# Sums of squares by head in the first block: two products in rounded fp32 in place of one full fp32 product

## The chip, the cores and the metric

The kernel runs on one core of a Trainium2 chip. The metric is the time on the device of one launch, in microseconds (us). An engine of the core is written as the profile writes it: PE is the matrix engine TensorE (PEld its weight loads), DVE is VectorE, ACT is ScalarE, POOL is GpSimd, SP issues the transfers of weights.

## The reference

512 tokens of width 1024 go through two blocks. The change touches the first one, whose queries and keys are normalized head by head before the attention:

```python
proj = rmsnorm(x, ln1_g) @ w_in
qa, ka, va, qb, kb, vb, ga, gb = split(proj)
qa = rope(rmsnorm_by_head(qa, q_norm_a))      # 12 heads of 64, as ka
qb = rope(rmsnorm_by_head(qb, q_norm_b))      # 8 heads of 64; kb has 2
oa = dilated_attention(qa, ka, va)
ob = banded_attention(qb, kb, vb, 127, sinks)
mix = sigmoid(ga) * (oa @ w_branch_a) + sigmoid(gb) * (ob @ w_branch_b)
x = x + mix @ w_out
# then x + relu(rmsnorm(x) @ w_up)**2 @ w_down, and a second block of another kind
```

`rmsnorm_by_head` divides each head's 64 values by the root of their mean square, in fp32.

## The kernel before

Activations lie transposed: a tile has 128 features on the partitions and 512 tokens beside each other. A "head" of the program (`head_chain`) is one such tile with two heads of 64 in it. There are 17 in the first block: one for kb, four for qb, six each for qa and ka.

**The dense work** is done with numbers split in two: weights and activations are each rounded to a high part (type fp32r) and the rest is kept as a low part, and a block of 128x128 weights costs three products of 128x512 (high by high, high by low, low by high). A group, 8 blocks and 24 products, makes one tile of a projection. Weights come by transfer in units of 8 blocks; ACT rounds the unit (`half_weights`, L1679), POOL subtracts in four quarters (L1992), and PE waits for each quarter. Group by group the result is taken from the bank by DVE (`proj`, L1197).

**A head** goes through these steps. `head_in`: DVE multiplies by gain and cosine (L1203) and shuffles a copy (L1204), while ACT squares the tile (L1749). `head_sum`: PE multiplies the squares by `bones`, a 128x128 matrix of ones in two blocks of 64, which puts each head's sum on all of its rows; it is one product in full fp32. `head_rope`: DVE, L1211 and L1213. `head_rs`: ACT takes logarithm, exponential and square (L1710, L1712, L1715). `head_newton`: DVE, L1219 and L1222. `head_out`: POOL multiplies (L2000). The chain has three tiles and two banks for itself, a **slot**, and there are three slots.

**Attention** works in the same three slots. 16 items of banded attention (`swa_item`, four query tiles by four blocks of rows) each take scores, softmax (DVE L1282, L1285 and three tiny steps from L1288, then L1298, L1301 and L1305 twice), a transposition (L875), values and a copy (L1310). 8 dilated items (`dil_item`) are some three times as large (L1246, L1252, L1262, L1270 on DVE, L841 on PE), and the first four need all of six heads, the last four all of six others.

**The order of the work** is made when the program is built. `Schedule` keeps a clock for each engine by costs of its own, puts a slot's next step into the program as soon as its inputs would be there, and puts dense groups between. A free slot takes the next head if one waits, and only otherwise an attention item:

```python
def fill(self):
    for i, g in enumerate(self.slots):
        queue = self.side if i == len(self.slots) - 1 else self.heads or self.waiting
```

The dense groups of this stage are the 17 tiles of the heads and 16 gates. The gates are kept back where their tiles lie on memory that attention still uses:

```python
for k in range(2):
    gate1(k)
sch.until(*[(n, t_) for n in ("qa", "ka") for t_ in (1, 3, 5)])
heads_done = tuple(slot_head.values())
for k in range(2, 11):
    gate1(k, heads_done)
```

In the same way the gates 11 to 13 wait in the order for `until("oa0")`, the first four dilated items, gate 14 for `until("oa")`, all eight, and gate 15 for the last attention item. On the chip each engine goes through its instructions in the order that was planned, whatever the real times are.

## Time and profile before

| | us |
|---|---|
| median of 3 runs (lowest, highest) | 2407.05 (2406.53, 2407.55) |
| profiled execution, span | 2406.4 |
| PE busy | 2379.8 (99%) |
| PEld busy | 1924.6 (80%) |
| DVE busy | 1209.2 (50%) |
| ACT busy | 965.8 (40%) |
| POOL busy | 1316.2 (55%) |

The span of the profiled execution is its time from first to last instruction, 0.7 us under the median. The page cuts it into 40 slices of 60 us. PE is busy in nine tenths of each slice but the first; the granted clock is full in all of them (mean 0.998). DVE has 5 in the first slice, then 9 and 9, then 7, and between 2 and 7 afterwards. The first block's attention runs from 58 to 330 us. The chain of work that ended last is 91% PE, 6% DVE.

### The profile page before, as it was taken

Reading aid. Unit: us, or ns where it says so; the run is one execution under the profiler, and the core shown is the slowest. Engines: PE = TensorE matmul, PEld = TensorE weight load, DVE = VectorE, ACT = ScalarE, POOL = GpSimd, SP = SyncE. Lnnn points to the kernel's source line nnn. Section 1 sums busy time; section 2 is a strip of 40 time slices with the busy share of each in tenths; the row PEclk is TensorE's granted clock in tenths of the full one; section 3 lists DMA queues with packets and bytes.
Section 4 is the critical chain, followed back from the end, with each engine's and each line's share of the span. In section 5 each row is a group of like instructions: output and inputs, shape, how many; then the busy total and the mean of one; then the engine's idle time right before and its main releaser. Section 6 shows DMA issues by size and latency. Waiting matters only on the chain.

```text
span 2406.4 us, 29717 instructions
## 1 busy us (share of the span) xinstructions
PE 2379.8 (99%) x11108; PEld 1924.6 (80%) x11108; DVE 1209.2 (50%) x1961; ACT 965.8 (40%) x1513; POOL 1316.2 (55%) x1589
## 2 busy tenths in 40 slices
PE   8999999999999999999999999999999999999999
PEld 8777778888888888777787888888887777788887
DVE  5997765423224432379625743333325785266331
ACT  4554444322223223566524432332336764344321
POOL 5763246656556655366244765555554562466554
PEclk9999999999999999999999999999999999999999
DMA  5321123333333333222122333333332221223333
GB/s 166 109 71 53 47 77 97 96 97 97 97 97 110 97 97 103 71 72 69 54 87 79 97 97 97 96 97 97 97 98 67 72 78 53 88 87 98 96 97 96
DMA packets 59758, 213.40 MB, mean 89 GB/s; under 512 B 6624, under 2 KB 6752, under 8 KB 59488
## 3 DMA queue, kind: packets, MB, share of 16 engines
q1 hardware_dynamic: 59472, 211.38, 29.2%
q8 instruction: 88, 1.44, 0.2%
q14 instruction: 54, 0.44, 0.1%
q10 hardware_dynamic: 144, 0.14, 0.0%
HBM read 209.39 MB, written 2.10 MB: 88 GB/s over the span
## 4 chain that ended last, share of the span: by engine, by line
PE 91%; DVE 6%; issue 1%; ACT 1%; DMA 0%; POOL 0%; SPq 0%; DVEq 0%; ACTq 0%
PE banks L721 89%; DVE t L1203 1%; DVE t L1211 1%; DVE t L1213 1%; DVE t L1488 1%; DVE t L1204 1%; DVE t L1197 1%; DVE t L1219 0%; PE banks L841 0%; PE banks L995 0%; DVE t L1222 0%; ACT t L1679 0%; DMA t<-in_w 0%; PE banks L875 0%; POOL t L1992 0%
## 5 line engine op out<-in xcount | busy, mean ns | idle before, releaser
L721 PE MATMUL banks<-t,t 128*128 128x512 f32 (+4 forms) x10788 | 2351.7, 387 | 17.2 <-ACT t L1699 5.9
L721 PEld LDWEIGHTS banks<-t,t 128*128 128x128 f32 (+2 forms) x10788 | 1889.5, 188 | 452.2 <-issue 64.3
L1992 POOL TENSOR_TENSOR t<-t,t 128x256 fp32r<-128x256 f32 x1544 | 1258.9, 846 | 1049.9 <-ACT t L1679 1041.5
L1679 ACT ACTIVATE t<-t 128x1024 fp32r<-128x1024 f32 x385 | 408.2, 1060 | 1078.8 <-issue 605.5
L1197 DVE TENSOR_TENSOR t<-banks,t 128x512 f32<-128x512 f32 x121 | 83.1, 687 | 169.8 <-PE banks L721 169.2
L1378 DVE TENSOR_TENSOR t<-banks,t 128x512 f32<-128x512 f32 x44 | 30.4, 690 | 184.5 <-PE banks L721 184.3
L1346 DVE SCALAR_TENSOR_TENSOR t<-banks,t 128x512 f32<-128x512 f32 x32 | 22.1, 691 | 155.4 <-PE banks L721 155.4
L1080 DVE SCALAR_TENSOR_TENSOR t<-t,t,t 128x512 fp32r<-128x512 f32 x64 | 52.0, 817 | 58.1 <-ACT t L1699 58.1
L1323 DVE TENSOR_TENSOR t<-t,t 128x512 fp32r<-128x512 f32 x68 | 70.5, 1036 | 2.3
L1352 DVE TENSOR_TENSOR t<-banks,t 128x512 f32<-128x512 f32 x24 | 16.6, 691 | 106.0 <-PE banks L721 106.0
L1699 ACT ACTIVATE t<-t,t 128x512 fp32r<-128x512 f32 x64 | 45.6, 715 | 55.7 <-DVE t L1346 49.1
L2000 POOL TENSOR_TENSOR t<-t,t 128x512 f32<-128x512 f32 x33 | 49.6, 1506 | 29.7 <-DVE t L1222 29.7
L1373 DVE TENSOR_TENSOR t<-banks,t 128x512 f32<-128x512 f32 x44 | 30.4, 691 | 70.3 <-PE banks L721 69.9
L1093 DVE TENSOR_TENSOR t<-t,t 128x512 f32<-128x512 f32 x56 | 59.4, 1061 | 3.1 <-ACT t L1705 3.1
L1321 DVE CAST t<-t 128x512 fp32r<-128x512 f32 x68 | 55.3, 813 | 2.5
L1358 DVE SCALAR_TENSOR_TENSOR t<-banks,t 128x512 f32<-128x512 f32 x32 | 22.1, 691 | 65.2 <-PE banks L721 65.1
L1344 DVE TENSOR_TENSOR t<-banks,t 128x512 f32<-128x512 f32 x32 | 22.1, 690 | 56.6 <-PE banks L721 56.6
L1488 DVE SCALAR_TENSOR_TENSOR t<-t,t,t 128x511 f32<-128x511 f32 (+2 forms) x48 | 46.7, 972 | 7.1 <-ACT t L1887 6.3
L1715 ACT ACTIVATE t<-t 128x512 f32<-128x512 f32 x45 | 28.5, 633 | 33.4 <-DVE t L1213 32.5
L1710 ACT ACTIVATE t<-banks,t 128x512 f32<-128x512 f32 x45 | 30.6, 681 | 22.5 <-PE banks L721 22.4
L1098 DVE SCALAR_TENSOR_TENSOR t<-banks,t 128x512 f32<-128x512 f32 x12 | 8.3, 692 | 57.8 <-ACT t L1715 57.7
L1705 ACT ACTIVATE t<-t 128x512 f32<-128x512 f32 x56 | 34.6, 617 | 4.8 <-DVE t L1093 4.8
(182 smaller groups left out, 1304.7 us busy)
## 6 DMA issues: line engine op xcount, KB each, us to landing
t<-in_w SPq DMA_DIRECT2D x386, 512.0 KB, 3.5
t<-in_xT SPq DMA_DIRECT2D x8, 256.0 KB, 5.7
out<-t SPq DMA_DIRECT2D x8, 256.0 KB, 4.5
t<-in_dmask SPq DMA_DIRECT2D x1, 1536.0 KB, 7.7
t<-in_vbias SPq DMA_DIRECT2D x2, 384.0 KB, 4.1
t<-in_c SPq DMA_DIRECT2D x1, 576.0 KB, 8.6
t<-in_w SPq DMA_DIRECT2D x2, 256.0 KB, 3.9
t<-in_pos SPq DMA_DIRECT2D x2, 256.0 KB, 4.1
```

Source lines behind the costliest of these rows:

```text
L721: return pe.matmul(o, l, r, start=start, stop=stop, skip_group_check=True)
L1080: v.scalar_tensor_tensor(out=XL[m], in0=X[m], scalar=g, in1=as_f32(XH[m]), op0=M_, op1=S_).then_inc(*v_norm.next(("xl", s, m)))
L1093: v.tensor_tensor(acc, acc, sqt, A_).then_inc(*v_norm.next(("acc", s, m)))
L1197: v.tensor_tensor(G.dst, B[G.bank], rstdB, M_).then_inc(*v_evac.next(("proj", g)))
L1321: v.tensor_copy(hi, src).then_inc(*v_evac.next())
L1323: v.tensor_tensor(lo, src, as_f32(hi), S_).then_inc(*v_evac.next(name))
L1488: v.scalar_tensor_tensor(out=dst[:, tap:S], in0=T[k][:, 0:S - tap], scalar=cols_t[:, cw + 3 - tap:cw + 4 - tap], in1=dst[:, tap:S], op0=M_ ...
L1679: a.activation(whl[u % 2][:, 0:1024], wraw[u % 3][:, :], ACT.Copy).then_inc(*w_high.next(u))
L1699: a.activation(XH[m], X[m], ACT.Copy, scale=col(STAGE[s], m)).then_inc(*a_norm.next(("high", s, m)))
L1705: a.activation(sqt, X[m], ACT.Square).then_inc(*a_norm.next(("square", s, m)))
L1992: p.tensor_tensor(hl[:, 1024:2048][:, c], wraw[u % 3][:, c], as_f32(hl[:, c]), ALU.subtract).then_inc(*w_low.next((u, q)))
L2000: p.tensor_tensor(H["R"], b_, a, ALU.mult).then_inc(*p_attn.next(("head", hid)))
```

## The change

For the 17 heads of the first block ACT squares the tile twice: once to fp32, as before, and once rounded to fp32r (`SQH`). DVE subtracts the two and writes the rest as fp32r (`SQL`), a new step `head_split`. PE then makes two products with a rounded copy of `bones`, one for each part, into the same bank. The copy of `bones` is made once on DVE in `turns1`, in memory that the second block's `consts` fills later; `consts` waits for the 17 sums. `SQH` and `SQL` lie in the slot's attention tiles. The second block's heads (gains of table 2) stay as they were.

```diff
+        SQH = [reg(88 + 6 * s, S, F32R)[:, :] for s in range(3)]
+        SQL = [reg(91 + 6 * s, S, F32R)[:, :] for s in range(3)]
+        bones_r = mask_r[:, 0:128]
...
             def head_sum(hid):
                 H = heads[hid]
                 ba = pair(H["slot"])[0]
+                if H.get("table") == 1:
+                    need.wait_ge(*v_norm.at(("bones",)))
+                    need.wait_ge(*a_attn.at(("square_high", hid)))
+                    need.wait_ge(*v_attn.at(("square_low", hid)))
+                    free(ba)
+                    mm(B[ba], bones_r, SQH[H["slot"]], True, False)
+                    mm(B[ba], bones_r, SQL[H["slot"]], False, True).then_inc(*t_attn.next(("sum", hid)))
+                    bank[ba] = [(v_attn, ("summed", hid))]
+                    return
...
+                v.tensor_copy(bones_r, C["bones"]).then_inc(*v_norm.next(("bones",)))
...
+            def head_split(hid):
+                H = heads[hid]
+                a = H["tiles"][H["slot"]][0]
+                need.wait_ge(*a_attn.at(("square_high", hid)))
+                reach(need, *H["tile_free"])
+                v.tensor_tensor(SQL[H["slot"]], a, as_f32(SQH[H["slot"]]), S_).then_inc(*v_attn.next(("square_low", hid)))
...
                 a.activation(a_, H["R"], ACT.Square).then_inc(*a_attn.next(("square", hid)))
+                if H["table"] == 1:
+                    reach(need, *H["tile_free"])
+                    a.activation(SQH[H["slot"]], H["R"], ACT.Square).then_inc(*a_attn.next(("square_high", hid)))
...
-                put("head_in", hid)
-                yield "t", (a_attn, ("square", hid))
+                if k["table"] == 1:
+                    k["tile_free"] = list(slot_busy[slot])
+                    put("head_in", hid)
+                    yield "v", (a_attn, ("square_high", hid))
+                    put("head_split", hid)
+                    yield "t", (v_attn, ("square_low", hid))
+                else:
+                    put("head_in", hid)
+                    yield "t", (a_attn, ("square", hid))
                 put("head_sum", hid)
```

The planned order moves with it. The first place is DVE, between the evictions of two neighbouring groups (L1197, in the change L1212) in the middle of the heads. Before (the next eviction follows):

```order
L1197 TENSOR_TENSOR t_101<-banks,t_57 128x512
L1298 TENSOR_TENSOR t_67<-t_67 128x2
L1301 RECIPROCAL t_67<-t_67 128x2
L1305 TENSOR_SCALAR t_124<-t_124,t_67 128x256 x2
L1203 SCALAR_TENSOR_TENSOR t_167<-t_104,t_66,t_56 128x512
L1204 STREAM_SHUFFLE t_168<-t_104 128x512
L1310 COPY t_123<-banks 128x128
L1211 SCALAR_TENSOR_TENSOR t_168<-t_168,t_62,t_56 128x512
L1213 TENSOR_TENSOR t_167<-t_167,t_168 128x512
L1310 COPY t_64<-banks 128x128
L1203 SCALAR_TENSOR_TENSOR t_164<-t_110,t_66,t_56 128x512
L1204 STREAM_SHUFFLE t_165<-t_110 128x512
```

With the change (L1218 and L1219 are `head_in`, L1226 the subtraction, L1233 and L1235 `head_rope`, L1241 and L1244 `head_newton`):

```order
L1212 TENSOR_TENSOR t_101<-banks,t_57 128x512
L1233 SCALAR_TENSOR_TENSOR t_171<-t_171,t_62,t_56 128x512
L1235 TENSOR_TENSOR t_170<-t_170,t_171 128x512
L1226 TENSOR_TENSOR t_135<-t_172,t_132 128x512
L1212 TENSOR_TENSOR t_107<-banks,t_57 128x512
L1241 SCALAR_TENSOR_TENSOR t_171<-banks,t_171 128x512
L1244 SCALAR_TENSOR_TENSOR t_169<-t_171,t_169 128x512
L1233 SCALAR_TENSOR_TENSOR t_174<-t_174,t_62,t_56 128x512
L1235 TENSOR_TENSOR t_173<-t_173,t_174 128x512
L1218 SCALAR_TENSOR_TENSOR t_167<-t_110,t_66,t_56 128x512
L1219 STREAM_SHUFFLE t_168<-t_110 128x512
L1212 TENSOR_TENSOR t_103<-banks,t_57 128x512
```

The attention steps between them (L1298 to L1310) have moved to behind the heads; from the first eviction to the last `head_newton` five banded items have passed their copy L1310 before, and one with the change.

The second place is PE, around the last head's sum, just ahead of gate 2. Dense products are `t_50` with `t_54` or `t_55`. Before, a head's sum is `t_160`, `t_163` or `t_166` with `t_58`, the scores of banded items are `t_117` with another, those of dilated ones `t_106`, and L875 is a transposition:

```order
L721 MATMUL banks<-t_166,t_58 128x512
L721 MATMUL banks<-t_50,t_55 128x512 x18
L721 MATMUL banks<-t_50,t_54 128x512 x3
L721 MATMUL banks<-t_163,t_58 128x512
L721 MATMUL banks<-t_50,t_54 128x512 x3
L721 MATMUL banks<-t_117,t_114 128x256 x2
L721 MATMUL banks<-t_50,t_54 128x512 x18
L721 MATMUL banks<-t_106,t_100 128x512 x2
L721 MATMUL banks<-t_160,t_58 128x512
L875 MATMUL banks<-t_58,t_128 128x128 x4
L721 MATMUL banks<-t_50,t_55 128x512 x15
L721 MATMUL banks<-t_129,t_118 64x128 x4
```

With the change a sum is a pair, `t_130` to `t_132` and then `t_133` to `t_135`, each with `t_63`; the last row is gate 2:

```order
L724 MATMUL banks<-t_131,t_63 128x512
L724 MATMUL banks<-t_134,t_63 128x512
L724 MATMUL banks<-t_132,t_63 128x512
L724 MATMUL banks<-t_135,t_63 128x512
L724 MATMUL banks<-t_117,t_114 128x256 x2
L724 MATMUL banks<-t_117,t_115 128x256 x2
L724 MATMUL banks<-t_130,t_63 128x512
L724 MATMUL banks<-t_133,t_63 128x512
L724 MATMUL banks<-t_50,t_55 128x512 x24
```

The sums of the last three heads now stand in a row, with no dense product between them. Ahead of the last sum there stood six scores, five transpositions and five values of banded items and one pair of a dilated item's scores; now it is three, one, one and none.

The third place is PE between gates 13 and 15. Before, from late in gate 13 on, the steps of the last banded items stand singly between dense rows, up to the first product of the branch outputs:

```order
L721 MATMUL banks<-t_50,t_54 128x512 x12
L875 MATMUL banks<-t_58,t_124 128x128 x4
L721 MATMUL banks<-t_50,t_55 128x512 x6
L875 MATMUL banks<-t_58,t_128 128x128 x4
L721 MATMUL banks<-t_117,t_116 128x256 x2
L721 MATMUL banks<-t_125,t_118 64x128 x4
L721 MATMUL banks<-t_129,t_118 64x128 x4
L721 MATMUL banks<-t_50,t_55 128x512 x18
L875 MATMUL banks<-t_58,t_126 128x128 x4
L721 MATMUL banks<-t_127,t_118 64x128 x4
L721 MATMUL banks<-t_50,t_54 128x512 x24
```

With the change, 134 products of attention stand in a row between gates 13 and 14, of which this is the beginning (`t_107` to `t_111` are scores of dilated items, L853 their transpositions, 64x128 their values). They hold the transpositions and values of four dilated items, all of the scores of one of these, and four scores, three transpositions and two values of banded items:

```order
L724 MATMUL banks<-t_50,t_54 128x512 x15
L853 MATMUL banks<-t_58,t_124 128x128 x4
L853 MATMUL banks<-t_58,t_125 128x128 x4
L853 MATMUL banks<-t_58,t_128 128x128 x4
L853 MATMUL banks<-t_58,t_129 128x128 x4
L853 MATMUL banks<-t_58,t_124 128x128 x2
L853 MATMUL banks<-t_58,t_125 128x128 x2
L724 MATMUL banks<-t_109,t_103 128x128 x2
L724 MATMUL banks<-t_111,t_105 128x128 x2
L853 MATMUL banks<-t_58,t_128 128x128 x2
L853 MATMUL banks<-t_58,t_129 128x128 x2
L724 MATMUL banks<-t_124,t_112 64x128
```

The longest row without a dense product had 48 before, between groups of gates. From the branch outputs on, the order is the same.

## Rows read from the trace of the kernel before

**Rows 1.** The page: busy time of the engines over the whole span.
```profile
PE 2379.8 (99%) x11108; PEld 1924.6 (80%) x11108; DVE 1209.2 (50%) x1961; ACT 965.8 (40%) x1513; POOL 1316.2 (55%) x1589
...
DVE  5997765423224432379625743333325785266331
```

**Rows 2.** Windows: heads, rest of attention, dense products; busy us by engine.
```profile
58.50:189.00 130.50, 126.20 (x554) 92.24 (x553) 121.76 (x195) 69.87 (x120) 89.30 (x88) 1.00 0.29 91
189.00:330.00 141.00, 138.47 (x890) 106.82 (x891) 100.22 (x235) 62.60 (x139) 43.71 (x58) 1.00 0.18 53
330.00:400.00 70.00, 70.00 (x310) 58.01 (x309) 45.97 (x59) 29.80 (x41) 45.36 (x52) 1.00 0.31 91
```

**Rows 3.** Order of time, PEld: weight loads around the first head's sum (start, us).
```profile
60.29 0.35 PEld L721 LDWEIGHTS banks<-t,t 128*128 128x128 f32 x2
60.88 0.19 PEld L721 LDWEIGHTS banks<-t,t 128*128 128x128 f32 x1 [0.24 <-issue]
61.31 0.42 PEld L721 LDWEIGHTS banks<-t,t 128*128 128x128 f32 x2 [0.24 <-issue]
```

**Rows 4.** Groups of instructions on DVE, 58.5 to 196.5 us (busy us, mean ns).
```profile
L1305 DVE TENSOR_SCALAR t<-t,t 128x256 f32<-128x256 f32 x12 | 8.0, 703 | 0.2
L1282 DVE SCALAR_TENSOR_TENSOR t<-banks,t 128x256 f32<-128x256 f32 x12 | 4.5, 411 | 0.0
L1285 DVE TENSOR_REDUCE t<-t 128x2 f32<-128x512 f32 x6 | 4.1, 686 | 0.2
L1298 DVE TENSOR_TENSOR t<-t 128x2 f32<-128x2 f32 x6 | 2.9, 480 | 0.0
L1288 DVE TENSOR_TENSOR t<-t,t 128x2 f32<-128x2 f32 x6 | 2.1, 358 | 0.2
L1310 DVE COPY t<-banks 128x128 f32<-128x128 f32 x6 | 1.6, 279 | 0.3 <-PE banks L721 0.3
```

**Rows 5.** Groups of instructions on ACT, 58.5 to 189 us: the squares.
```profile
L1749 ACT ACTIVATE t<-t 128x512 f32<-128x512 f32 x17 | 10.5, 617 | 0.7 <-POOL t L2000 0.5
```

**Rows 6.** One line, L1213, 60 to 330 us: duration in ns, min/median/max.
```profile
L1213 DVE TENSOR_TENSOR t<-t,t x17: 691/1110/1664, 61.9 to 192.2; 128x512 f32<-128x512 f32 x17
```

**Rows 7.** Order of time around the last head's sum, PEld.
```profile
188.84 0.30 PEld L721 LDWEIGHTS banks<-t,t 128*128 128x128 f32 x2 [0.66 <-ACT t L1749]
...
191.10 0.42 PEld L875 LDWEIGHTS banks<-t,t 128*128 128x128 f32 x4 [1.97 <-DVE t L1305]
...
191.49 2.15 PEld L721 LDWEIGHTS banks<-t,t 128*128 128x128 f32 x10
```

**Rows 8.** Order of time, PEld: a banded item's scores, then another's values.
```profile
91.55 0.30 PEld L721 LDWEIGHTS banks<-t,t 64*128 64x128 f32 x4 [0.35 <-issue]
92.18 0.30 PEld L721 LDWEIGHTS banks<-t,t 128*128 128x128 f32 x2 [0.33 <-issue]
...
137.84 0.42 PEld L721 LDWEIGHTS banks<-t,t 128*64 128x64 f32 x8 [0.17 <-issue]
138.43 1.00 PEld L721 LDWEIGHTS banks<-t,t 128*128 128x128 f32 x5 [0.17 <-issue]
```

**Rows 9.** Waits, 58.5 to 330 us (us in total, times, longest us).
```profile
POOL t L1992 <- ACT t L1679: 122.9, 27, 12.8
...
PEld banks L721 <- POOL t L1992: 0.7, 3, 0.2
```

**Rows 10.** Order of time: first and last step of the last dilated item.
```profile
290.80 1.29 DVE L1246 SCALAR_TENSOR_TENSOR t<-banks,t 128x512 f32<-128x512 f32 x2 [2.34 <-PE banks L721]
...
314.79 0.38 ACT L1791 ACTIVATE t<-banks 128x128 f32<-128x128 f32 x1
```

**Rows 11.** Groups of instructions on DVE, 189 to 330.2 us: dilated items.
```profile
L1252 DVE TENSOR_REDUCE t<-t 128x1 f32<-128x768 f32 x16 | 14.5, 947 | 0.3
L1262 DVE TENSOR_SCALAR t<-t,t 128x768 f32<-128x768 f32 x16 | 10.8, 672 | 0.6
L1246 DVE SCALAR_TENSOR_TENSOR t<-banks,t 128x512 f32<-128x512 f32 x16 | 10.2, 681 | 3.6 <-PE banks L721 3.6
```

More of the change, by code:

```diff
@@ L677, in build_program @@
         groups, stage_end, wide_of = [], {}, {}
-        heads = {}
+        heads, heads_first = {}, []
         dil_at, swa_at, gates1, merge1 = {}, {}, {}, {}
@@ L1114, in consts @@
                 need.wait_ge(*in_cols.at("cols"))
+                for hid in heads_first:
+                    need.wait_ge(*t_attn.at(("sum", hid)))
                 v.tensor_copy(mask_r[:, 0:128], C["ident"]).then_inc(*v_norm.next())
@@ L1644, in vector_program @@
                     "rope_angles": rope_angles, "values1": values1, "proj": proj, "head_in": head_in, "key_rope": key_rope,
-                    "head_rope": head_rope, "head_newton": head_newton, "dil_soft": dil_soft, "dil_norm": dil_norm,
+                    "head_split": head_split, "head_rope": head_rope, "head_newton": head_newton, "dil_soft": dil_soft, "dil_norm": dil_norm,
                     "dil_pt": dil_pt, "swa_soft": swa_soft, "swa_norm": swa_norm, "swa_out": swa_out,
@@ L2239, in head1 @@
             src = proj(n, 0, R, rope1)
+            heads_first.append((n, t_))
             sch.heads.append(head_chain((n, t_), R=R, g=col(n), table=1, turned=TURNED[n], ones=C["bones"], n=64,
```

## The prediction

> **What bounds the kernel now.** The page first: PE is busy in 99% of the span and DVE in 50%, but DVE's digits have two slices with a 9, from 60 to 180 us, which is where the heads are [rows 1]. So an average says little here, and the windows are read next. With the heads (58.5 to 189 us) PE is busy for 126.2 of 130.5 us and DVE for 121.8; in the rest of the attention (to 330 us) PE for 138.5 of 141.0, DVE for 100.2; behind that PE alone counts [rows 2]. The first stage thus has two engines that are both nearly full, and the change takes work from one and gives it to the other.
>
> **What PE gains.** The loads around the first head's sum show a full fp32 product as two loads: the first begins 0.19 us before the end of its row, at 60.45, the second at 60.88, and the next dense product's at 61.31, so it takes 0.86 us [rows 3]. A dense product, of the same type and size as each of the two new ones, takes 70.0 / 310 = 0.226 us [rows 2]. Per head 0.86 - 0.45 = 0.41 us, for 17 heads 6.9 us less on PE. That would be the whole story if PE alone counted.
>
> **What ACT and POOL get.** ACT gets 17 squares of 0.62 us [rows 5], 10.5 us, beside 69.9 us of work in 130.5 [rows 2]. It has room, and the square stands early in a chain that is over 10 us long; three slots need to give a head only every 7.7 us (130.5 / 17). I cost it at nothing. If that cover goes, weights are rounded later, since they stand behind it on ACT. POOL gets nothing, but waits 122.9 us for ACT's rounding between 58.5 and 330 us, and PE waited for POOL for only 0.7 us [rows 9], so a late square of 0.6 us is taken up there.
>
> **What DVE gets in the stage of the heads.** 17 subtractions of two tiles of 128x512 that both lie in SBUF. The nearest row is L1213, same size and kind: 0.69 at least, 1.11 median, 1.66 at most [rows 6]. I take the median: 18.9 us. The cast of `bones` and one shuffle that now comes before the last sum are together about 1 us. But the order also takes work out of this stage. Five softmax fronts go behind the heads (L1282 twice, L1285 and three tiny steps, no longer than L1288: 0.82 + 0.69 + 1.07 = 2.58 us each), four backs (L1298 and L1305 twice: 1.89 us) and four copies (0.28 us) [rows 4]: 12.9 + 7.5 + 1.1 = 21.5 us. Net, DVE has 18.9 + 1.0 - 21.5 = -1.6 us up to the last head's sum. Its stage took 130.5 us for 121.8 us of work [rows 2], so by the same ratio the last sum, at 188.84 us before [rows 7], comes about **2 us earlier**. With the subtraction at 0.69 us it would be 9 us earlier, with 1.66 us 8 us later; these are the bounds.
>
> So nothing of the 6.9 us is seen here. PE has 126.2 - 6.9 us less what was moved behind (next part), about 110 us of work, in a stage that DVE makes 128 us long: some 18 us of waiting, most of it where three sums stand in a row ahead of gate 2, with all dense products that may stand there used up.
>
> **What PE gets behind the heads.** The steps that were moved are three scores, four transpositions, four values of banded items and a pair of dilated scores. With the idle time ahead, scores take 0.35 + 0.63 us and values 0.17 + 0.59 us [rows 8]; a transposition takes 0.39 us [rows 7]; the dilated pair has no row and is taken as the scores. Together 2.9 + 1.6 + 3.0 + 1.0 = 8.5, so **+9 us** (6 us without the idle times, 11 us if each step costs 0.2 us more). In this stage PE was busy for 138.5 of 141.0 us [rows 2], so all of it shows.
>
> **The row of 134 products between gates 13 and 14.** Here PE has no dense product to fill with, and DVE sets the pace. DVE's work in it: of dilated items 8 times L1262, 4 times L1252 and 4 wide L1246 [rows 11] are 5.4 + 3.8 + 2.7 us; 4 narrower L1246 and 8 copies from the banks, taken as L1282 [rows 4], 4.9 us; four whole softmaxes and three copies of banded items, at most 4 x 4.47 + 0.8 = 18.7 us. In all at most 35.5 us; the banded part is priced by the crowded stage, so I take 33. The end of it runs beside gate 14 (24 x 0.226 = 5.4 us), which leaves 27 us to PE. PE's own work in it, by the durations above, is 19 us (60 transpositions at 0.39 per four, 56 values at 0.59 per four, 4 scores at 0.63 and 2 us for the dilated scores). So **+8 us** of waiting. Least is 0, as before nothing of this size shows there. Most is the chain: the fourth dilated item starts when the first has given its values, and the last one took 24.4 us from its scores' arrival to its end (290.80 to 315.17) [rows 10], with 7 us ahead of it 31 us, so +12.
>
> **Sum.** -2 + 9 + 8 = +15 us on the profiled execution's 2406.4, which lies 0.7 us under the median of 2407.05: **2422 us**, 0.6% slower. Everything behind 330 us stands in the same order and is taken as unchanged; `consts` waits for sums that are long past.
>
> **A rule against my price.** The rows show L1213 at 0.69 or at 1.11 us and more, with nothing in between explained by its size [rows 6]. The Trainium skill, page "SBUF — State Buffer", section "SBUF: two separate sides", says that VectorE and GpSimd share a pair of ports that is locked for a whole instruction when VectorE has two inputs in SBUF, and that the loser waits. That fits a subtraction that often waits for one of POOL's quarters. By the rule the added subtraction makes POOL wait as well, and its price is 0.69 us plus luck; this gives the second rival below.
>
> **Rivals.**
> *Faster: only PE counts.* -6.9 us, 2400 us. It decides if DVE's queue up to the last sum is done within PE's own 110 us, and the row between gates 13 and 14 within PE's 19. For it: PE is the bound of the page. Against: DVE's 121.8 us of work less 1.6 us [rows 2], which would have to shrink by 10 us. Chance 0.05.
> *Cheap subtraction.* At 0.69 us each the last sum comes 9 us earlier: -9 + 9 + 8 = +8, 2415 us. For it: the least duration of the row, and that the order leaves fewer instructions to collide with. Chance 0.17.
> *The moved work fits.* Cheap subtraction, and DVE keeps up in the row of 134 products: -9 + 6 + 0 = -3 to +3, about 2407 us. For it: DVE has 40 us free behind the heads [rows 2]. Against: they are not in that row. Chance 0.09.
> *Collisions.* The subtraction at its dearest, POOL's quarters and so the weights late, the chain at its longest: +8 + 9 + 12 = +29, 2436 us. For it: three waits in a row on an engine that is full. Against: POOL waits for ACT so much [rows 9]. Chance 0.13.
> *The change isn't what it says*, one of the two products takes as long as a full one: 17 x 0.4 us more on PE, in a stage where PE waits anyway. It moves the time by less than the bounds do, and every dense product [rows 2] speaks against it.
>
> **How the numbers follow.** The forecast has 0.56. A measurement can tell about 0.2%, 4.8 us, from no change. Faster by more than that is only the first rival: 0.05. Within it is most of the case in which the moved work fits: 0.08. The rest, 0.87, is slower. The range takes in the cheap subtraction and nearly all of the collisions: 2409 to 2435 us.
>
> **What would show it.** Right: the last pair of products for a head at about 187 us; PE busy for some 110 of 130 us in the stage of the heads, its waits ended by DVE's subtraction; the new DVE line with 17 instructions of 1.0 to 1.1 us; gate 13 evicted near 305 us and gate 14 some 33 us later; PE's waits there ended by DVE; the first product of the branch outputs at about 345 us in place of 330; the same 2076 us behind it. Wrong: if PE doesn't wait in the heads, the step on DVE's queue fails; if the row of 134 products runs in 20 us, the third term fails; if the time behind the branch outputs moves, something isn't here at all.

## The result and the profile after

| | before | after |
|---|---|---|
| median (lowest, highest) of 4 runs each, us | 2406.79 (2405.76, 2407.55) | 2427.26 (2426.25, 2428.98) |
| profiled execution, span, us | 2406.4 | 2424.6 |

The change makes the kernel slower: 1.0081 times the time before, with an interval from 1.0069 to 1.0093; the medians lie 20.5 us apart. The forecast was 2422, with 2409 to 2435 as its range. All medians here and below are of fast runs, so one run of 9181 us (of e11) and one of 3937 us (of e12) are left out of them.

The page of the kernel after, busy time over the whole span and DVE's digits. Against [rows 1] PE is busy as long as before, which is one per cent less of the span; PE's line in the costliest groups now shows 31.2 us of idle time where it showed 17.2.

```profile
PE 2380.2 (98%) x11108; PEld 1928.3 (80%) x11108; DVE 1218.8 (50%) x1979; ACT 975.3 (40%) x1530; POOL 1324.6 (55%) x1589
...
DVE  5996766423224432378634843333325785266330
...
L724 PE MATMUL banks<-t,t 128*128 128x512 f32 (+5 forms) x10788 | 2349.5, 386 | 31.2 <-ACT t L1771 6.1
```

The windows of [rows 2], for the kernel after (the columns are window, its length, busy time and instructions of PE, PEld, DVE, ACT and POOL, granted clock, DMA share, GB/s):

```profile
58.50:189.00 130.50, 115.88 (x492) 89.52 (x491) 123.03 (x169) 71.22 (x110) 99.40 (x92) 0.95 0.30 94
189.00:330.00 141.00, 130.85 (x838) 99.00 (x836) 101.23 (x252) 62.52 (x150) 37.34 (x49) 0.98 0.15 46
330.00:400.00 70.00, 68.48 (x334) 56.02 (x335) 46.24 (x75) 30.05 (x49) 33.70 (x40) 0.98 0.23 69
```

With the heads PE is busy for 10 us less than before and DVE for 1 us more. Behind them PE has waits where it had nearly none.

Four moments of DVE's queue say where the time went: the first head's eviction, the last step of the last head (`head_newton`), and the evictions of gates 13, 14 and 15. In order of time, before:

```profile
58.61 0.69 DVE L1197 TENSOR_TENSOR t<-banks,t 128x512 f32<-128x512 f32 x1 [2.72 <-PE banks L721]
...
195.71 0.69 DVE L1222 SCALAR_TENSOR_TENSOR t<-t,t 128x512 f32<-128x512 f32 x1
...
313.58 0.69 DVE L1197 TENSOR_TENSOR t<-banks,t 128x512 f32<-128x512 f32 x1
...
322.18 0.69 DVE L1197 TENSOR_TENSOR t<-banks,t 128x512 f32<-128x512 f32 x1 [0.99 <-PE banks L721]
...
330.21 0.69 DVE L1197 TENSOR_TENSOR t<-banks,t 128x512 f32<-128x512 f32 x1 [0.49 <-PE banks L721]
```

and after:

```profile
58.21 0.69 DVE L1212 TENSOR_TENSOR t<-banks,t 128x512 f32<-128x512 f32 x1 [2.72 <-PE banks L724]
...
193.52 0.69 DVE L1244 SCALAR_TENSOR_TENSOR t<-t,t 128x512 f32<-128x512 f32 x1
...
301.09 0.69 DVE L1212 TENSOR_TENSOR t<-banks,t 128x512 f32<-128x512 f32 x1 [0.33 <-PE banks L724]
...
342.04 0.69 DVE L1212 TENSOR_TENSOR t<-banks,t 128x512 f32<-128x512 f32 x1 [2.12 <-PE banks L724]
...
350.05 0.69 DVE L1212 TENSOR_TENSOR t<-banks,t 128x512 f32<-128x512 f32 x1 [0.47 <-PE banks L724]
```

Two stretches are read from them for every run below. **Heads** is first eviction to last newton: 137.1 us before, 135.3 after, so -1.8. **Behind** is last newton to gate 15: 134.5 before, 156.5 after, so +22.0. Inside it the way to gate 13 is 10.3 us shorter and the stretch from gate 13 to 14 grows from 8.6 to 41.0 us. What follows gate 15 takes 2076.2 and 2074.6 us.

The waits of the kernel after in the heads' stage (us in total, times, longest):

```profile
PEld banks L724 <- ACT t L1771: 7.2, 3, 5.5
PE banks L724 <- ACT t L1771: 6.1, 2, 5.1
...
PE banks L724 <- DVE t L1226: 5.7, 6, 1.8
```

The first two rows name ACT's plain square (L1771), which no sum of the change waits for: a sum waits for the rounded square (L1774) and the subtraction (L1226) of its own head. The longest of these waits, in order of time, shows what it was:

```profile
174.44 0.62 ACT L1774 ACTIVATE t<-t 128x512 fp32r<-128x512 f32 x1
...
178.93 1.20 DVE L1226 TENSOR_TENSOR t<-t,t 128x512 fp32r<-128x512 f32 x1
...
179.64 0.61 ACT L1771 ACTIVATE t<-t 128x512 f32<-128x512 f32 x1
...
180.16 0.61 ACT L1774 ACTIVATE t<-t 128x512 fp32r<-128x512 f32 x1
180.25 0.50 PEld L724 LDWEIGHTS banks<-t,t 128*128 128x128 f32 x2 [5.47 <-ACT t L1771]
```

The head's rounded square was there at 175.06. The squares at 179.64 and 180.16 are the next head's; the second of them ended at 180.77, when PE was already at work. What this sum waited for is its subtraction, which ended at 180.13, as in the other wait put down to L1771 (the subtraction ended at 165.76, the load began at 165.88). So 5.7 + 6.1 = 11.8 us of PE's waits with the heads are ended by the subtraction.

The chain of work that ended last, in the row without dense products, shows how that row runs (start us, us, what):

```profile
301.89 0.62 DVE t L1284
...
308.89 1.81 DVE t L1274 x2
310.70 0.67 DVE t L1292 x2
311.42 2.71 PE banks L724 x28
314.13 1.02 PE banks L853 x8
...
319.26 1.81 DVE t L1274 x2
...
321.38 0.63 DVE t L1327 x2
```

It passes from DVE to PE and back, since an item's transposition, softmax and values each wait for the step before. Nothing stands between for PE to do meanwhile.

### The profile page after: what moved, and what is told of

It reads as the page before. It is cut to its first block, busy times and chain, and to the rows that moved or that the text cites. A ratio compares the mean times of both kernels' runs of the same rounds, so it can differ in the third digit from the quotient of the medians.

```text
span 2424.6 us, 29769 instructions
## 1 busy us (share of the span) xinstructions
PE 2380.2 (98%) x11108; PEld 1928.3 (80%) x11108; DVE 1218.8 (50%) x1979; ACT 975.3 (40%) x1530; POOL 1324.6 (55%) x1589
## 4 chain that ended last, share of the span: by engine, by line
PE 88%; DVE 3%; issue 1%; ACT 1%; POOL 1%; DVEq 0%; ACTq 0%
PE banks L724 86%; PE banks L853 0%; PE banks L1007 0%; POOL t L2017 0%; PE banks L887 0%; DVE t L1218 0%; ACT t L1701 0%; DVE t L1510 0%; POOL t L2025 0%; DVE t L1244 0%; DVE t L1233 0%; DVE t L1212 0%; DVE t L1219 0%; DVE t L1235 0%; PE banks L1063 0%
## 5 line engine op out<-in xcount | busy, mean ns | idle before, releaser
L724 PE MATMUL banks<-t,t 128*128 128x512 f32 (+5 forms) x10788 | 2349.5, 386 | 31.2 <-ACT t L1771 6.1
L1212 DVE TENSOR_TENSOR t<-banks,t 128x512 f32<-128x512 f32 x121 | 83.0, 686 | 165.8 <-PE banks L724 163.8
```

The source lines that it names most:

```text
L724: return pe.matmul(o, l, r, start=start, stop=stop, skip_group_check=True)
L1212: v.tensor_tensor(G.dst, B[G.bank], rstdB, M_).then_inc(*v_evac.next(("proj", g)))
```

## The experiments

Two theories stood at first. **D**: VectorE's time paces the heads' stage, as predicted. **O**: what counts is the order, in two ways, TensorE standing in order at a head's sum, and attention steps driven behind the heads. A third, **P**, is that each microsecond of TensorE's work counts. Here are all 12 kernels, each with its ratio to the kernel before in runs on the same chip (its median there was 2408.19 us beside e1 to e4, 2406.72 beside e5 to e8, 2407.71 beside e9 to e12) and the two stretches read as above, in us:

| run | us, median | ratio (interval) | heads | behind |
|---|---|---|---|---|
| before | 2406.79 | | 137.1 | 134.5 |
| the change | 2427.26 | 1.0081 (1.0069 to 1.0093) | 135.3 | 156.5 |
| e1_old_order | 2441.19 | 1.0138 (1.0125 to 1.0152) | 165.9 | 137.2 |
| e2_full_product | 2431.87 | 1.0101 (1.0086 to 1.0117) | 136.3 | 158.1 |
| e3_high_part_only | 2415.30 | 1.0026 (1.0016 to 1.0037) | 129.4 | 148.4 |
| e4_pool_subtracts | 2453.69 | 1.0189 (1.0175 to 1.0203) | 150.5 | 167.4 |
| e5_work_not_awaited | 2417.34 | 1.0050 (1.0036 to 1.0064) | 146.5 | 136.3 |
| e6_longer_chain | 2413.72 | 1.0028 (1.0017 to 1.0039) | 141.7 | 135.5 |
| e7_filled_waits | 2428.66 | 1.0089 (1.0075 to 1.0102) | 135.5 | 155.3 |
| e8_subtract_at_once | 2426.87 | 1.0080 (1.0067 to 1.0093) | 133.4 | 157.0 |
| e9_new_order_alone | 2423.53 | 1.0067 (1.0054 to 1.0079) | 131.5 | 157.0 |
| e10_relieved_before | 2403.85 | 0.9986 (0.9977 to 0.9995) | 133.5 | 135.4 |
| e11_relieved_old_order | 2437.55 | 1.0125 (1.0110 to 1.0141) | 164.2 | 138.9 |
| e12_high_part_old_order | 2411.65 | 1.0014 (1.0005 to 1.0023) | 137.6 | 138.0 |

### Old order, full product, high part alone, GpSimd

**e1_old_order**: the planner doesn't see the new steps, so they stand in the order of the kernel before.

```diff
                if k["table"] == 1:
                     k["tile_free"] = list(slot_busy[slot])
                     put("head_in", hid)
-                    yield "v", (a_attn, ("square_high", hid))
                     put("head_split", hid)
-                    yield "t", (v_attn, ("square_low", hid))
+                    yield "t", (a_attn, ("square", hid))
```

> All instructions of the change, but in the order of before: the planner is given no time for the second square and the subtraction and the old time for the sum, so each engine's instructions stand as before, with the new ones put in. Theory D (DVE's queue paces the heads): DVE has the 17 subtractions, 18 us, in the stage of the heads and nothing is moved out of it, so the last head's sum comes some 13 us later than before (about 202 us); behind it PE has the same work as before and no bare row, so the whole is +13 us, about 2420 us, some 7 us under the change. Rival O (the moved order alone costs): with the old order the time is that of before or up to 7 us under it, 2400 to 2407 us.

Measured: 33 us over the kernel before, 28.8 of them in the heads' stage. Both theories missed it: D had +13 us, O at most none. VectorE's work alone doesn't explain it. In the waits, from 58.5 to 227 us:

```profile
PE banks L724 <- DVE t L1238: 24.4, 13, 3.0
DVE t L1221 <- PE banks L724: 21.0, 13, 2.8
```

PE stands at 13 sums for the subtraction (L1238), up to 3.0 us each; then DVE stands for the evictions of products (L1221) that PE made late because of it. Two queues in order lose the same time in turn.

**e2_full_product**: the change and its order, with one full fp32 product in place of the two (the planner still reckons with the two).

```diff
-                    mm(B[ba], bones_r, SQH[H["slot"]], True, False)
-                    mm(B[ba], bones_r, SQL[H["slot"]], False, True).then_inc(...)
+                    mm(B[ba], H["ones"], H["tiles"][H["slot"]][0]).then_inc(...)
```

> The change with its squares, subtractions and order, but PE makes the old full fp32 product of the fp32 squares at the place of the two products; the rounded parts are made and waited for, not used. So PE gets its 17 x 0.4 = 6.9 us back. Theory D: PE waits for more than that in the stage of the heads, so 0 to +3 us against the change, about 2429 us. Rival P (each us of PE counts): +7 us, 2434 us.

Measured: 4.6 us over the change by the medians, 3.2 if each is taken against the kernel before in its own series. In the profiled executions 1.0 us lies in the heads' stage and 1.6 behind; the rest is in the start of the first head, which differs between 58 and 61 us from kernel to kernel, and in the tail. So of TensorE's 6.9 us some 2.5 are seen in the two stretches. The medians alone don't part D's bound of 3 from P's 7, since the two intervals overlap; the stretches speak for D.

**e3_high_part_only**: one product of the rounded square, no subtraction. It leaves out the low part of the squares.

```diff
-                    need.wait_ge(*v_attn.at(("square_low", hid)))
                     free(ba)
-                    mm(B[ba], bones_r, SQH[H["slot"]], True, False)
-                    mm(B[ba], bones_r, SQL[H["slot"]], False, True).then_inc(...)
+                    mm(B[ba], bones_r, SQH[H["slot"]]).then_inc(...)
```

> Leaves out the low part: ACT makes the rounded square alone, no subtraction, one product per head, so the sums are those of rounded squares. PE has 17 x 0.63 = 10.7 us less than before, DVE and ACT have the same as before. Theory D: DVE's queue still paces the heads, so of the 10.7 us only 0 to 4 are seen; about 2404 us. Rival P: -10.7 us, 2396 us.

Measured: 7 us slower than before, against both expectations, though TensorE has 10.7 us less to do and VectorE only the cast of `bones` more. The heads' stage is 7.7 us shorter, the stretch behind it 13.9 longer: the planner, told of cheaper sums, wrote another order again. This run turned the study to the order.

**e4_pool_subtracts**: the subtraction on GpSimd.

```diff
-                v.tensor_tensor(SQL[H["slot"]], a, as_f32(SQH[H["slot"]]), S_).then_inc(*v_attn...)
+                p.tensor_tensor(SQL[H["slot"]], a, as_f32(SQH[H["slot"]]), ALU.subtract).then_inc(*p_attn...)
```

> The change, but POOL makes the subtraction (some 1.5 us each, 25 us beside 89 us of its work in the stage of the heads). DVE is relieved of 18 us, but the planner moves all banded items behind the heads and leaves the same row of 134 products without a dense one. Theory D with its second part (moved work and the bare row cost by themselves): the last sum comes 5 us or more earlier than with the change (under 182 us), the rest of the attention costs as much or 2 us more, so 2420 to 2427 us. Rival: if DVE's added 18 us are all there is, 2405 to 2410 us.

Measured: 26 us over the change, outside both expectations, with VectorE free for a third of the stage. VectorE's busy time doesn't set this stage: PE stands for 21.2 us at three sums for GpSimd's subtraction, which waits behind GpSimd's quarters of the weights. From the start of `head_in` on VectorE to the end of `head_out` on GpSimd a head takes 24.2 us, the mean of 17 (17.1 in the change, 11.8 before). That a long chain costs by itself isn't shown: in e8 the mean is 14.7 us at the change's time, and in e9 it is 17.0 us with a shorter heads' stage than before.

### The work, the chain, the clock, the place in the queue

**e5_work_not_awaited**: order and products of the kernel before; rounded square, difference and cast are done, but no sum waits for them.

```diff
                 if H.get("table") == 1:
-                    need.wait_ge(*a_attn.at(("square_high", hid)))
-                    need.wait_ge(*v_attn.at(("square_low", hid)))
+                    need.wait_ge(*a_attn.at(("square", hid)))
...
-                v.tensor_tensor(SQL[H["slot"]], a, as_f32(SQH[H["slot"]]), S_)
+                v.tensor_tensor(SQL[H["slot"]], as_f32(SQH[H["slot"]]), as_f32(SQH[H["slot"]]), S_)
```

> The kernel before and its order, with all the work that the change adds put in where it would stand in that order (the rounded square on ScalarE, a difference of two 128x512 tiles on VectorE behind each of the 17 heads' first two VectorE instructions, the cast of bones), but nobody waits for any of it: the heads' sums stay full fp32 products of the plain square, behind the plain square alone. It tells what the work costs by itself. Theory D (VectorE's time paces the heads' stage): 17 x 1.11 = 19 us of VectorE work are added to 122 of 130 us and nothing is moved out, so some +13 us on the kernel before. Theory O (the run with the old order lost its 33 us to TensorE standing in order at each sum for the subtraction, and the change loses its 20 us to the new order): 0 to +5 us.

Measured: +10.6 us, +9.4 in the heads' stage. The group of the difference, 58.5 to 210 us:

```profile
L1230 DVE TENSOR_TENSOR t<-t 128x512 fp32r<-128x512 f32 x17 | 11.9, 701 | 0.8 <-ACT t L1780 0.8
```

It was cheaper than the 1.11 us of D's sum. If all of the 9.4 us come from it, four fifths of its 11.9 us show, and VectorE's queue paces that stage in the old order; ScalarE's 17 added squares are in the same run and were not parted from it. Of e1's 33 us some 10.6 are the work, and some 22 come only when the sum waits for it.

**e6_longer_chain**: the kernel before with two more squares on ScalarE ahead of the awaited one.

```diff
+                if H["table"] == 1 and not isinstance(a, Planned):
+                    a.activation(SQH[H["slot"]], H["R"], ACT.Square)
+                    a.activation(SQL[H["slot"]], H["R"], ACT.Square)
                 a.activation(a_, H["R"], ACT.Square).then_inc(*a_attn.next(("square", hid)))
```

> The kernel before and its order, with two more squares on ScalarE ahead of the one that a head's sum waits for: each head's chain is longer by 2 x 0.62 = 1.2 us on ScalarE, which has 60 us free in this stage; no work is added to VectorE, TensorE or GpSimd, and the order is as it was. It leaves out nothing. If the length of a head's chain alone decided in a given order (theory O, TensorE stands in order at each sum): at most 17 x 1.2 = +20 us, less where a sum was not late. If VectorE's time decides (D): within 2 us of the kernel before, since the sum stands far enough behind the square.

Measured: +7 us, +4.6 in the heads' stage, for 1.2 us more in each of 17 chains on an engine that has room. D alone would have given nothing. So work on ScalarE ahead of a head's awaited square isn't free. (In the change the added square stands behind the plain one.)

**e7_filled_waits**: the change with dummy dense products in PE's waits.

```diff
+            def filler(n, bk):
+                free(bk)
+                for i in range(n):
+                    mm(B[bk], XH[0][:, 0:128], XH[0])
...
+                    filler(FILL_SUM.get(fill["sums"], 0), ba)
                     need.wait_ge(*a_attn.at(("square_high", hid)))
```

> The change, with dummy products of the dense kind (0.226 us each) put where TensorE waited in the change's profile: 37 ahead of the last four heads' sums (2.1, 5.5, 2.8 and 0.8 us of waiting there) and 48 in the row without dense products between gates 13 and 14; they write banks that are free and are overwritten, nothing else reads them. They measure what the lowered granted clock behind the waits costs (0.50 at 180 to 190 us and 0.83 at 320 to 340 us in the change's profile). If the waits are all that is lost and the clock matters little: the change's time within 2 us, or up to 4 us longer where a filler is still running when its wait would have ended. If the lowered clock stretched the work behind the waits: the granted clock stays near 1 in those windows and the time falls by some 3 to 6 us, to 2421 to 2424.

Two windows, 170 to 180 us and from gate 13 to 14, of PE alone (window, length, busy time, granted clock, DMA share, GB/s), first of the change:

```profile
170.00:180.00 10.00, 3.46 (x15) 0.82 0.23 71
301.00:342.00 41.00, 30.94 (x243) 0.92 0.05 14
```

then of e7:

```profile
170.00:180.00 10.00, 10.00 (x45) 1.00 0.33 105
301.00:342.00 41.00, 40.36 (x295) 1.00 0.05 14
```

PE is now busy without a break and at full clock there, and the time is the change's (+1.4 us, inside both intervals). PE's waits are what the row's length leaves over, and neither they nor the lowered clock made it: those 41 us belong to the chains over DVE and ACT. The first expectation holds. In the heads' stage the dummy products took half of the waits (PE idle for 7.1 us in place of 14.6) and the stage was as long (135.5 against 135.3). From 180 to 190 us PE was busy for only 6.84 us and the clock fell to 0.74, so there a cost of the clock stays untested.

**e8_subtract_at_once**: the subtraction right behind the head's first two instructions on VectorE.

```diff
                     put("head_in", hid)
-                    yield "v", (a_attn, ("square_high", hid))
                     put("head_split", hid)
```

> The change, but the subtraction is put into VectorE's queue right behind the head's first two instructions and not as a step of its own: a head's chain has one turn in VectorE's queue less, VectorE may instead stand and wait for ScalarE's rounded square. The same operations, the planner sees them. If the length of the chains (three slots held longer) is what drives steps behind the heads and so the time: chains shorter than the change's 17.1 us, more banded steps ahead of the last sum, and 3 to 10 us faster than the change. If VectorE's time is what counts: the same or 0 to 5 us slower, since VectorE now also waits.

Measured: the change's time (-0.4 us); 1.9 us gained with the heads, 0.5 lost behind, the rest at the start. A head's chain is 14.7 us in place of 17.1. Neither the turn in VectorE's queue nor the length of the chain is what costs here.

### The order alone, and relief

**e9_new_order_alone**: the order is planned for the change, the operations issued are those of the kernel before.

```diff
-                if H.get("table") == 1:
+                if H.get("table") == 1 and PLANNING[0]:
                     need.wait_ge(*v_norm.at(("bones",)))
...
             def head_split(hid):
+                if not PLANNING[0]:
+                    return
...
-                if H["table"] == 1:
+                if H["table"] == 1 and PLANNING[0]:
                     reach(need, *H["tile_free"])
                     a.activation(SQH[H["slot"]], H["R"], ACT.Square).then_inc(...)
```

> The change's order of steps on every engine, with the operations of the kernel before in it: each head has its one plain square and its full fp32 product, there is no rounded square, no subtraction and no cast of bones. It leaves out nothing. It tells what the new order costs by itself. From the run with the high part alone (new order of its own, no VectorE work, 8.6 us over the kernel before), and since the heads' stage loses 19 us of VectorE work: last head's sum 6 to 9 us earlier than in the kernel before, the stretch behind it some 18 us longer; +8 to +12 us in all, and so the work and its waits in that order are the other 8 to 12 of the change's 20. If the order is harmless and the work alone counts: -8 to 0.

Measured: +15.8 us, more than the 8 to 12 expected, so 15.8 of the change's 20.5 us come with the order alone. (The two intervals overlap a little; the stretches below place the rest.) Behind the heads it is the change again (157.0 against 156.5). In order of time, gates 13 and 14:

```profile
297.87 0.69 DVE L1224 TENSOR_TENSOR t<-banks,t 128x512 f32<-128x512 f32 x1 [0.33 <-PE banks L735]
...
338.77 0.69 DVE L1224 TENSOR_TENSOR t<-banks,t 128x512 f32<-128x512 f32 x1 [2.12 <-PE banks L735]
```

40.9 us, as in the change. The heads' stage is 5.6 us shorter than before, though VectorE is busy in it for 13 us less (115.2 against 128.3), and the chain of work from 58.5 to 189 us says why: in the kernel before

```profile
by line: PE banks L721 28.7%; DVE t L1203 9.2%; DVE t L1211 9.1%; DVE t L1213 7.5%; DVE t L1219 6.3%; DVE t L1204 6.2%; issue 6.0%; DVE t L1222 4.8%; DVE t L1197 4.8%; POOL t L1992 3.1%; ACT t L1715 2.0%; DVE t L1305 2.0%; DVE t L1282 1.6%;
```

and in e9

```profile
by line: PE banks L735 86.2%; issue 3.3%; POOL t L2031 2.5%; DVE t L1230 2.1%; DVE t L1247 1.4%; POOL t L2039 1.3%; DVE t L1231 1.1%; ACT t L1715 0.8%; DVE t L1249 0.6%; DVE t L1255 0.5%; PE banks L898 0.3%; DVEq L214 0.0%
```

With the moved steps gone from VectorE, TensorE becomes the bound for most of the stage (busy for 124.0 of 131.5 us), so only 5.6 us are gained. The change then puts 17.2 us of subtractions on VectorE and takes 6.9 from TensorE: 3.8 us back, which is the rest of its loss but for a microsecond.

**e10_relieved_before**: VectorE's product by the sine table over 64 of 512 columns, in the kernel before. It leaves out that part of the rotation, and so does the next.

```diff
-                v.scalar_tensor_tensor(out=c, in0=c, scalar=H["turned"], in1=SIN, op0=M_, op1=M_)...
+                n_ = 64 if H["table"] == 1 and not isinstance(v, Planned) else 512
+                v.scalar_tensor_tensor(out=c[:, 0:n_], in0=c[:, 0:n_], scalar=H["turned"], in1=SIN[:, 0:n_], op0=M_, op1=M_)...
```

> The kernel before and its order, but VectorE's product of the turned head by the sine table (1.17 us on 128x512) runs over 64 of the 512 columns: VectorE has 17 x 1.0 = 17 us less to do in the heads' stage. It leaves out that part of the rotation. It is the base for the run with the same relief and the change's operations. If VectorE's time paces the stage (D): 5 to 10 us faster, then TensorE (126 of 130 us) is the bound. If the chains' turns in a fixed order decide (O): 0 to 3 us faster.

Measured: -3.9 us. The groups of that line, 58.5 to 196 us, of the kernel before and of e10:

```profile
L1211 DVE SCALAR_TENSOR_TENSOR t<-t,t,t 128x512 f32<-128x512 f32 x17 | 19.9, 1170 | 0.4
```

```profile
L1212 DVE SCALAR_TENSOR_TENSOR t<-t,t,t 128x64 f32<-128x64 f32 x17 | 12.3, 721 | 0.4
```

An eighth of the columns took six tenths of the time, so the relief was 7.6 us and not 17. It shortened the heads' stage by 3.6 us, half of what was taken away, and the run by 3.9, between the 0 to 3 of O and the 5 to 10 that D expected for 17 us.

**e11_relieved_old_order**: the same relief in e1 (same edit as e10).

> The run e1_old_order (all operations of the change, in the order of the kernel before, +33 us) with the relief of e10_relieved_before: VectorE's product by the sine table over 64 of 512 columns, so that VectorE has as much work as in the kernel before. It leaves out that part of the rotation. D (the 33 us come from VectorE's queue being late at each sum): within 5 us of the kernel before, 8 to 12 us over e10. O (TensorE stands at each sum for one more turn of a chain, however full VectorE is): 20 us and more over e10, 2418 or more.

Measured: +29.8 us over before, 33.7 over e10; the relief took 1.6 us from e1's heads' stage. With the relief smaller than meant D's test is weaker, but its 8 to 12 us over e10 is far off: TensorE's standing in order at the sums is what e1 pays for, as O says.

**e12_high_part_old_order**: the order of the kernel before, one rounded square, one one-pass product. It leaves out the low part of the squares.

```diff
-                mm(B[ba], H["ones"], H["tiles"][H["slot"]][0]).then_inc(...)
+                mm(B[ba], *((bones_r, SQH[H["slot"]]) if H.get("table") == 1 and not PLANNING[0] else (H["ones"], ...))).then_inc(...)
...
+                if H["table"] == 1 and not PLANNING[0]:
+                    reach(need, *H["tile_free"])
+                    a.activation(SQH[H["slot"]], H["R"], ACT.Square).then_inc(*a_attn.next(("square", hid)))
```

> The order of the kernel before on every engine; for the 17 heads one rounded square in place of the plain one and one one-pass product in place of the full fp32 product, and nothing on VectorE but the cast of bones. It leaves out the low part of the squares, which the sum of squares then lacks. TensorE has 17 x (0.86 - 0.23) = 10.7 us less to do and no chain is longer. It tells what TensorE's gain is worth where nothing is given for it. If VectorE paces the stage (D, the prediction's step): 0 to -3 us on the kernel before. If TensorE does: -8 to -11 us.

Measured: +3.9 us (1.0014, interval 1.0005 to 1.0023), so no gain and a small loss, outside both expectations. TensorE's 10.7 us buy nothing, and the heads' stage stays at 137.6 us, as D's step has it; PE only stands longer in it (13.4 us idle in place of 5.4). The loss shows behind the heads, 138.0 against 134.5. PE alone in that stretch, before and in e12:

```profile
195.71:330.21 134.50, 133.11 (x864) 1.00 0.18 52
197.63:335.61 137.98, 136.59 (x881) 1.00 0.17 51
```

It has 17 products more to do there at full clock, at 0.226 us each 3.8 us: products that PE had done before the last newton in the kernel before. So the loss was made at the end of the heads' stage. PE waited more there, and its windows show a lowered clock:

```profile
160.00:180.00 20.00, 17.42 (x81) 1.00 0.26 73
180.00:200.00 20.00, 14.20 (x47) 0.74 0.20 59
200.00:220.00 20.00, 20.00 (x111) 1.00 0.10 28
```

How much of the 3.5 us is the clock and how much the waits, both in the same window, was not tried apart.

No run beat the kernel before with the whole computation in it.

## Why the prediction was right, point by point

- **The sum.** -2 + 9 + 8 = +15 was forecast, +20.5 measured (18.2 by the two profiled spans), inside the range. By the stretches: -1.8 with the heads, where -2 was forecast, +22.0 behind, where 17 was, and -2.0 from start and tail together.
- **PE's 6.9 us not seen.** Right in kind. e12 gives TensorE 10.7 us in the old order and the heads' stage doesn't move; e2 shows 1 us of the 6.9 in that stage and 2.5 in both stretches.
- **ACT's square at nothing.** Not tried by itself. In the change VectorE never sat idle ahead of the subtraction, so the rounded square was always there in time. e6 is a warning only: 1.2 us ahead of each awaited square cost 7 us in the old order.
- **The subtraction at 1.11 us.** Right: 17 instructions, median 1.14, in all 17.2 us against 18.9 forecast.
- **Last sum 2 us earlier, at about 187.** It stood at 186.73; the stage is 1.8 us shorter. The net of -1.6 us on DVE was near (busy for 127.6 us of the stage against 128.3), but "by the same ratio" hid two steps that nearly cancel: the moved work out gives 5.6 us and stops at TensorE (e9), the subtraction in costs 3.8. That the term came out at -2 is partly luck. And a microsecond of VectorE's work is worth less than one: 0.5 in e10 (3.6 of 7.6), at most 0.8 in e5 (9.4 of 11.9).
- **PE's waits in the heads' stage ended by the subtraction.** Right: 11.8 us, of which the profile puts 6.1 down to the next head's square. PE was busy for 115.9 us and not 110, at a mean granted clock of 0.95.
- **Moved steps +9 us, the row of 134 products +8 us.** From the last newton to gate 15 PE's idle time grows from 1.4 us (119.10 - 119.04 and 16.60 - 15.27 in the windows before) to 11.7 (0.4 up to 301 us, 10.1 from there to 342, 1.3 behind), so +10.3 us of waiting against 8 forecast. The other 11.7 of the 22.0 are work of PE: the moved steps, 9 forecast, and what the lowered clock stretches. Gate 13 to 14 took 41.0 us against "some 33": PE's own work without gate 14 is 30.9 - 5.4 = 25.5 us where 19 was taken from the durations, partly at a clock of 0.92. That term was mis-sized, and DVE's chains, not its 33 us of work, set the length: DVE was busy for 28.9 of the 41 us.
- **Branch outputs at about 345.** Gate 15 was evicted at 350.05 against 330.21. Gate 13 came 4 us earlier than the forecast 305 (301.09) and the row took 8 us more than its 33, so two errors partly cancel here.
- **Behind it unchanged.** 2074.6 against 2076.2 us.
- **The ports.** The trace of the kernel after has the subtraction at 0.67 us six times and at 1.1 to 1.4 ten times, with one at 0.96. In e1, where it stands elsewhere, its median is 0.67. Same instruction, same size: the price is in what runs beside it. The Trainium skill, page "SBUF — State Buffer", section "SBUF: two separate sides", has VectorE and GpSimd share ports under a lock held for an instruction when VectorE has two inputs there. The trace agrees (last section), and so does e10, where 64 columns took 0.29 us at best and 0.72 in the mean.
- **Rivals.** *Only PE counts* fell with e12, where TensorE's 10.7 us come with nothing added but the cast of `bones`, and the run is no faster. *Cheap subtraction* was true in six of 17. *The moved work fits* fell in the row between the gates. *Collisions* asked for late weights; PE waited 1.5 us for them up to 345 us.

What the prediction didn't see is how it splits: it spoke of VectorE's work, and 15.8 of the 20.5 us come without any of the new operations, from an order that was planned for them. Which of the planner's decisions made that order wasn't tried apart.

## What to carry to other kernels

Where a planner writes the order, a new step costs twice, as work and as the order that it brings; run the new order with the old operations once, and the two are apart. An engine's busy share doesn't say that it sets the time: fill its waits with dummy work, and if the time stays, look at the chains. Before taking work from the fullest engine, see whether its neighbour in the same stage is as full: here the second took back all that the first was given.

## What had not been expected of the hardware

**A narrow instruction that isn't cheap.** VectorE's three-operand product over 64 columns took 0.72 us in the mean, against 1.17 over 512, with 0.29 as the least of its durations. It took 0.29 us in the two cases in which GpSimd ran nothing beside it and 0.62 us or more in the other 15, so most of its time was waiting, and narrowing it gained 7.6 us where 17 were meant.

**The price of meeting GpSimd.** The dearest of the change's 17 subtractions, with the instruction of GpSimd in which it began:

```profile
77.33 1.28 POOL L2025 TENSOR_TENSOR t<-t,t 128x512 f32<-128x512 f32 x1 [0.63 <-DVE t L1244]
...
77.78 1.39 DVE L1226 TENSOR_TENSOR t<-t,t 128x512 fp32r<-128x512 f32 x1
```

GpSimd had 0.83 us left, and the subtraction took that and 0.56 us more. So it was with all eleven that took over 0.9 us: GpSimd was in an instruction when they began, and each took what was left of it and some 0.55 us. The three beside which GpSimd ran nothing took 0.68 us.

**The granted clock falls behind waits.** In the kernel after it reads, for PE from 180 to 200 us:

```profile
180.00:190.00 10.00, 6.88 (x18) 0.50 0.15 52
190.00:200.00 10.00, 10.00 (x52) 0.99 0.02 3
```

0.50 is the lower of TensorE's two levels, 1.2 GHz. It came after 10 us in which PE was busy for 3.46 us. With dummy products in the waits (e7) it was 1.00 at 170 to 180 us and 0.74 behind. Where e7 brought it back to 1.00 that gained no time that could be measured, since the chains on the other engines were longer.
